# Scans later in their slot, other places for the last weight row and the output chunks, and weight chunks asked for on ScalarE's queue

## The reference, cut to what matters

```python
h = rmsnorm(x, norm_g)
proj = h @ w_in                                  # q, k, v and gate of 3 groups of 8 heads, 8 forget logits
o_sb = stick_breaking_attention(q_sb, k_sb, v_sb)            # group A, strictly causal
o_ch = chunked_attention(rmsnorm(q), rmsnorm(k), v, bias)    # group B, own chunk + 8 before
o_fx = forgetting_attention(rmsnorm(q), rmsnorm(k), v, log_sigmoid(f_logit + b))   # group C, causal
mixed = concat(o_sb * silu(g_sb), o_ch * silu(g_ch), o_fx * silu(g_fx))
out = x + mixed @ w_out
```

## Time and profile before

| | |
|---|---|
| median of 3 runs | 1035.27 us (1034.49 to 1035.57) |
| the profiled execution | 1032.46 us, span 1030.7 us |
| PE busy | 1002.0 us (97%) |
| weight loads of PE | 911.0 us (88%) |
| DVE busy | 702.4 us (68%) |
| ACT busy | 630.4 us (61%) |
| GpSimd busy | 125.9 us (12%) |
| q1, the queue of SP's DMAs | 36.5% of 16 engines' span |

### The profile page before, as it was taken

How to read it: one execution, slowest core, us unless ns; L and a number is a source line. 1 busy time by engine, 2 the same in 40 slices (tenths; PEclk the granted TensorE clock), 3 DMA queues, 4 the chain that set the end, 5 groups by cost and what they waited for, 6 DMA issues and landing times.

```text
span 1030.7 us, 16364 instructions
## 1 busy us (share of the span) xinstructions
PE 1002.0 (97%) x5688; PEld 911.0 (88%) x5688; DVE 702.4 (68%) x1418; ACT 630.4 (61%) x1230; POOL 125.9 (12%) x152
## 2 busy tenths in 40 slices
PE   6999999999999999999999999999999999999998
PEld 6989999899899998898998998998998997787887
DVE  5656685765856867767667757879889888877100
ACT  6676785766766868667767767656566556553000
POOL 1320211101202122112112101002011010000000
PEclk9999999999999999999999999999999999999999
DMA  8244151342431523414315214304304219732920
GB/s 254 84 129 131 29 153 51 82 121 50 121 98 40 152 56 83 123 42 111 96 52 131 74 32 107 78 22 108 77 21 121 73 52 257 202 123 82 346 100 34
DMA packets 118066, 105.51 MB, mean 102 GB/s; under 512 B 10048, under 2 KB 94024, under 8 KB 117984
## 3 DMA queue, kind: packets, MB, share of 16 engines
q1 hardware_dynamic: 115904, 104.43, 36.5%
q10 hardware_dynamic: 2080, 0.04, 0.1%
HBM read 62.44 MB, written 19.98 MB: 80 GB/s over the span
## 4 chain that ended last, share of the span: by engine, by line
PE 75%; DVE 13%; DMA 5%; ACT 3%; issue 2%; SPq 2%; POOL 0%; ACTq 0%; DVEq 0%; POOLq 0%
PE psP L1246 35%; PE psO L1329 7%; PE psP L1250 7%; PE psT L1311 6%; PE psS L1294 4%; PE psS L1295 4%; DVE rb L1150 3%; PE psP L1377 3%; PE psS L1377 3%; PE psP L1347 2%; DMA wraw<-in_w_in_dram 2%; DVE z L1153 2%; PE psO L1377 2%; DVE pt L1161 2%; PE psT L1268 2%
## 5 line engine op out<-in xcount | busy, mean ns | idle before, releaser
L1246 PE MATMUL psP<-big 128*128 128x384 f32 (+1 forms) x2304 | 475.3, 344 | 0.5 <-DVE big L1005 0.5
L1246 PEld LDWEIGHTS psP<-big 128*128 128x128 f32 x2304 | 397.5, 189 | 8.0 <-DVE big L1005 1.0
L1161 DVE TENSOR_TENSOR pt<-psT,pt 128x512 fp32r<-128x512 f32 (+1 forms) x224 | 143.4, 641 | 110.8 <-ACT pt L953 109.6
L953 ACT ACTIVATE pt<-psT 128x512 fp32r<-128x512 f32 (+1 forms) x224 | 124.7, 557 | 103.0 <-PE psT L1311 102.4
L1250 PE MATMUL psP<-big 128*128 128x512 f32 x576 | 156.0, 403 | 0.0
L1329 PE MATMUL psO<-pt,vst 128*128 128x512 f32 (+3 forms) x576 | 138.1, 339 | 12.3 <-DVE pt L1161 11.1
L1311 PE MATMUL psT<-identr,z 128*128 128x128 f32 x816 | 125.6, 273 | 0.0
L1329 PEld LDWEIGHTS psO<-pt,vst 128*128 128x128 f32 x576 | 100.4, 188 | 27.9 <-DVE pt L1161 14.7
L1250 PEld LDWEIGHTS psP<-big 128*128 128x128 f32 x576 | 102.4, 189 | 17.9
L1311 PEld LDWEIGHTS psT<-identr,z 128*128 128x128 f32 x816 | 103.1, 141 | 15.7
L1294 PE MATMUL psS<-stack 128*128 128x256 f32 (+3 forms) x288 | 97.2, 345 | 1.8 <-DVE small L1127 1.8
(11 more groups left out here) (114 smaller groups left out, 1133.4 us busy)
## 6 DMA issues: line engine op xcount, KB each, us to landing
stack<-stack SPq DMA_DIRECT2D x192, 128.0 KB, 2.3
wraw<-in_w_in_dram SPq DMA_DIRECT2D x90, 192.0 KB, 2.7
wraw<-in_w_in_dram SPq DMA_DIRECT2D x24, 256.0 KB, 3.8
mixed_scratch<-mst SPq DMA_DIRECT2D x24, 256.0 KB, 2.7
mixed_scratch<-gate SPq DMA_DIRECT2D x24, 256.0 KB, 3.2
wraw<-in_w_out_dram SPq DMA_DIRECT2D x24, 256.0 KB, 3.2
rb<-decay_scratch SPq DMA_DIRECT2D x8, 512.0 KB, 4.1
big<-mixed_scratch SPq DMA_DIRECT2D x8, 512.0 KB, 5.7
```

Of the source, the lines that this page charges most:

```text
L953: nc.scalar.activation(pt[:, ci % PTR, 0, 0:w], psT[:, m % NT, 0:w], ACT.Copy).then_inc(s_hi, 1)
L1161: nc.vector.tensor_tensor(pt[:, ci % PTR, 1, 0:w], psT[:, m % NT, 0:w], pt[:, ci % PTR, 0, 0:w].bitcast(F32), ALU.subtract).then_inc(s_eva ...
L1246: ins = nc.tensor.matmul(dst[:, 0:TOKW - first], hT[a][:, k, i * P:(i + 1) * P], wpair[b][:, k, first:TOKW], start=(k == 0 and q == 0), st ...
```

## The change

Seven edits, which stand together:

1. ACT issues the DMAs of the chunks from 11 on, in place of SP. At the step of chunk c (c > 8), *ahead of its own copy* of chunk c, it asks for chunk c + 2. The slot's wait stays the same: chunk c + 2 waits for DVE to be done with chunk c - 1. SP keeps the first 11 chunks.
2. The scans of the stick-breaking pairs (`weigh`) stand at 0.92 in place of 0.85.
3. Weights row 7 stands at slot 4.05 in place of 3.6, in pairs 4 to 10.
4. `wout` 6 to 15 start at slot 3.9 in place of 4.2.
5. `forget` 1 stands at slot 6.0 in place of 3.7.
6. `decay` 1 stands at slot 7.0 in place of 4.9.
7. `load_chunk` moves out of SP's program and takes the engine as an argument.

```diff
-AT = {'diag': -0.9, 'tail': 0.3, 'weigh': 0.85, 'recip': 0.9, ...}
+AT = {'diag': -0.9, 'tail': 0.3, 'weigh': 0.85, 'remain': 0.92, 'recip': 0.9, ...}
-BEHIND_TURN = {('weights', 2): 1.5, ('weights', 3): 1.9, ('weights', 4): 2.3}
+BEHIND_TURN = {('weights', 2): 1.5, ('weights', 3): 1.9, ('weights', 4): 2.3, ('weights', 7): 4.05}
-WOUT = [round(0.6 + 0.6 * c, 2) for c in range(SOON)] + [round(4.2 + 0.35 * c, 2) for c in range(EARLY - SOON)]
+WOUT = [round(0.6 + 0.6 * c, 2) for c in range(SOON)] + [round(3.9 + 0.35 * c, 2) for c in range(EARLY - SOON)]
-FORGET = {("forget", 1): 3.7, ("decay", 1): 4.9}
+FORGET = {("forget", 1): 6.0, ("decay", 1): 7.0}
...
-            timed.append((n + AT["weigh"], ("weigh", n)))
+            timed.append((n + AT["weigh" if n < NSOFT else "remain"], ("weigh", n)))
...
+        def load_chunk(c, eng):
...
+            if CPRIOR[c] >= 0:
+                eng.wait_ge(s_wlo, CPRIOR[c] + 1)
+            eng.dma_start(dst, src).then_inc(s_wld[CSLOT[c]], 16)
...
             for step in PLAN:
                 kind = step[0]
-                if kind in ("weights", "gatew", "wout"):
-                    c = CHUNK[step]
-                    if c >= KT:
-                        load_chunk(c + 3)
...
             for step in PLAN:
                 kind = step[0]
+                if kind in ("weights", "gatew", "wout") and CHUNK[step] > KT:
+
+                    load_chunk(CHUNK[step] + 2, act)
```

More of the change, by code:

```diff
@@ L153, in item_cost @@
     return 0
-AT = {'diag': -0.9, 'tail': 0.3, 'weigh': 0.85, 'recip': 0.9, 'rescale': 1.65, 'turn': 1.35, 'turns': 3.05, 'gather': 0.5, 'mix': 2.25}
+AT = {'diag': -0.9, 'tail': 0.3, 'weigh': 0.85, 'remain': 0.92, 'recip': 0.9, 'rescale': 1.65, 'turn': 1.35, 'turns': 3.05, 'gather': 0.5, 'mix': 2.25}
 OWN = {('sq', 1): 0.2, ('norm', 1, 0): 1.0, ('norm', 1, 1): 2.2, ('heads', 0, 1): 1.75, ('keys', 0, 1): 2.4, ('heads', 1, 0): 4.6, ('keys', 1, 0): 5.5, ('keys', 1, 1): 9.5, ('vsplit', 0, 1): 5.6, ('vsplit', 1, 1): 6.6, ('heads', 1, 1): 8.6}
 NEXT = {('weights', 0): 0.2, ('weights', 1): 0.6, ('weights', 2): 1.1, ('weights', 3): 1.6, ('weights', 4): 2.1, ('weights', 5): 2.6, ('weights', 6): 3.1, ('weights', 7): 3.6, ('gatew', 0): 6.3, ('gatew', 1): 7.3, ('sq', 0): 10.3, ('norm', 0, 0): 11.7, ('norm', 0, 1): 12.3, ('heads', 0, 0): 13.4, ('keys', 0, 0): 14.3, ('vsplit', 0, 0): 13.9, ('vsplit', 1, 0): 15.5}
-BEHIND_TURN = {('weights', 2): 1.5, ('weights', 3): 1.9, ('weights', 4): 2.3}
+BEHIND_TURN = {('weights', 2): 1.5, ('weights', 3): 1.9, ('weights', 4): 2.3, ('weights', 7): 4.05}
 KEYS_AT = 0.05
-WOUT = [round(0.6 + 0.6 * c, 2) for c in range(SOON)] + [round(4.2 + 0.35 * c, 2) for c in range(EARLY - SOON)]
+WOUT = [round(0.6 + 0.6 * c, 2) for c in range(SOON)] + [round(3.9 + 0.35 * c, 2) for c in range(EARLY - SOON)]
 FIRST_AT = 3.2
@@ L578, in build @@
         block = ctx.enter_context(nc.Block())
+        def load_chunk(c, eng):
+            if c >= len(CHUNKS):
+                return
+            step = CHUNKS[c]
+            if step[0] == "weights":
+                _, j, k = step
+                g, jj = divmod(ktile(j), PPG)
+                src = w_in[0, k * P:(k + 1) * P, g * 4 * WG:(g + 1) * 4 * WG].rearrange(
+                    "p (f c) -> p f c", f=4)[:, 0:3, jj * P:(jj + 1) * P]
+                dst = wplace[CSLOT[c]][:, 0:QKV].rearrange("p (f c) -> p f c", f=3)
+            elif step[0] == "gatew":
+                _, j, h = step
+                g, jj = divmod(ktile(j), PPG)
+                col = (g * 4 + 3) * WG + jj * P
+                src = w_in[0, h * HALF:(h + 1) * HALF, col:col + P].rearrange("(k p) c -> p k c", p=P)
+                dst = wplace[CSLOT[c]].rearrange("p (k c) -> p k c", k=4)
+            else:
+                pos, half = wout_at(step[1])
+                src = w_out[0, ktile(pos) * P:(ktile(pos) + 1) * P, half * HALF:(half + 1) * HALF]
+                dst = wplace[CSLOT[c]]
+            if CPRIOR[c] >= 0:
+                eng.wait_ge(s_wlo, CPRIOR[c] + 1)
+            eng.dma_start(dst, src).then_inc(s_wld[CSLOT[c]], 16)
@@ L580, in _ @@
         @block.sync
         def _(sp):
[L582 to L604, removed]
@@ L611, in _ @@
             for c in range(KT):
-                load_chunk(c)
+                load_chunk(c, sp)
             for t in range(2, TT):
```

## The result

The changed kernel takes 1045.59 us (median of 4 runs, 1044.83 to 1045.88), the kernel before 1034.88 beside it: ratio 1.0103, 95% interval [1.0089, 1.0116]. It is 10.7 us slower, where the prediction had 2.7. The profiled execution has a span of 1043.6 against 1030.7, so the traces differ by 12.9, of which some 2 us are the low profiled execution of before.

What follows compares the result with a forecast made beforehand. The prediction took the kernel as a PE stream with short stalls, ended by late evacuations. Its terms, +1.6 + 1.9 + 1.2 + 0.3 - 0.6 - 2.1 + 1.2 - 0.8 = +2.7, gave 1035.27 + 2.7 = 1038.0 us; range 1027 to 1041.5.

Steps and rivals of the forecast that it cites:

- The new wait, edit 1: ACT's wait and issue delay its copy and all behind it; SP's heads, keys, mix get earlier, counted as nothing.
- pairs 1 to 3: ACT's chunk copies wait for DVE, mostly in idle time: 0.4 per pair, +1.2 us (0 to 4); pair 4 alike, +0.3.
- Pair 11 (edits 2 and 4): Waits of 1.28 and 1.62 us go; held chunks leave 0.8 of the 2.9; with +2.0 in the tail, net +1.2.
- the cycle: Per chunk where chunks are close: 0.6 (ACT) + 0.65 (DVE) + 0.45 issue + some 0.1 semaphores = 1.8 us.
- Start: Start-up: ACT's copy of the second gate chunk waits for DVE, delaying PE's turn of x block 5: +1.6 us.
- Pair 0: Second copy waits for DVE's first subtraction, moving the first exponential 2.6 us and PE's turn to 64.0: +1.9 us.
- `forget`: `forget` 1 and `decay` 1 moved later: a stall of nearly the same size; gain 0 to 3.4 us, taken as 0.8.
- Forgetting pairs: Pairs 5 to 7: held row 5 copy costs 1.0 each, later row 7 removes PE's last wait; net -0.6 us.
- Pairs 8 to 10: Later scans save 1.5 us a pair, late row 7 hands back 0.5 to 1.0; -2.1 in all (-4.5 to 0).
- Tail: `wout` 16 to 23: each copy waits for DVE, last scan and final unit's turn later: +2.0 us (0 to 3.1).
- 3 (the holds add up): ACT and DVE lock over whole stretches of pair 11 and pairs 1 to 3: +7.4, 1042.7 us; chance 0.15 with another rival.

Runs made afterwards that it cites:

- changed_behind: The changed kernel, with ACT asking for chunk c + 2 behind its own copy of c instead of ahead of it: 1034.7 us, ratio 1.0009 to the kernel before.
- behind_copy: The kernel before with edit 1 alone, but ACT asks for chunk c + 2 behind its own copy of c: 1035.0 us, ratio 1.0008.
- hold_only: The kernel before, loads still on SP; ACT only waits for DVE to finish chunk c - 1 ahead of copying chunk c: 1039.0 us, ratio 1.0046.
- gate_on_sp: The kernel before with edit 1, except that SP still asks for the gate chunks at their old place: 1042.8 us, ratio 1.0081.
- gate_on_act: The kernel before with only the gate chunks asked for by ACT, two ahead; weights rows and `wout` stay on SP: 1045.1 us, ratio 1.0109.
- queue_only: Also called the queue alone: the kernel before with edit 1 and none of the new places: 1048.3 us, ratio 1.0134.
- times_only: The changed kernel with its chunk loads given back to SP, three ahead, all new places kept: 1029.0 us, ratio 0.9950 to the kernel before.
- wout_on_sp: The kernel before with edit 1, except that the `wout` chunks stay with SP: 1044.8 us, ratio 1.0103.
- wait_ahead_issue_behind: The kernel before with edit 1, the wait for DVE ahead of ACT's copy and only the DMA put behind it: 1038.4 us, ratio 1.0047.
- row7_scans_split: The kernel before, loads on SP; row 7 at 4.05 in forgetting pairs, 3.88 in pairs 8 to 10, scans at 0.92 there: 1023.2 us, ratio 0.9900.

## Why the prediction was wrong

The sign was right and the size was not. changed_behind parts the run into what the request's place ahead of the copy costs (the change less changed_behind) and all the rest (changed_behind less before). The prediction's terms part the same way: 12.1 for waits and issue ahead (in pair 11 the 2.0 of the tail and the 2.1 of gain that it let the loop take), and -9.4 for the new places.

| | start | 0 | 1 to 3 | 4 | 5 to 7 | 8 to 10 | 11, tail | sum |
|---|---|---|---|---|---|---|---|---|
| place ahead, predicted | +1.6 | +1.9 | +1.2 | +0.3 | +3.0 | 0 | +4.1 | +12.1 |
| measured | -0.2 | +2.1 | +1.2 | +0.7 | +3.1 | +0.4 | +4.5 | +11.8 |
| the rest, predicted | 0 | -0.8 | 0 | 0 | -3.6 | -2.1 | -2.9 | -9.4 |
| measured | +1.1 | +0.1 | +3.7 | +0.8 | -2.3 | -3.9 | +1.7 | +1.2 |

The sum for the place ahead came out (12.1 and 11.8), in part by luck: the 4.5 of pair 11 has 1.7 us of low clock in it that no term had, and at the start the wait is there in both kernels. Of the rest, the near fit in pairs 5 to 10 is not the prediction's mechanism: behind_copy has -2.2 and -3.6 there with none of the new places. And the rest of pair 0 is flattered by the low clock of before, 1.7 us. The loss that the prediction lacked came in two steps.

- *"What is behind SP's queue (heads, keys, mix) gets earlier, which no wait of PE asks for: I give it nothing."* This step of "The new wait, edit 1" failed. The queue was also an order: a chunk asked for behind the key copies in the same queue did not make them late. From a second queue it does, and the copies, with 1.06 us of slack, take 1.8 longer. That is the 3.7 of pairs 1 to 3: behind_copy has 3.3 with no wait ahead of the copy, hold_only has 0.1, gate_on_sp takes 1.0 a pair away in pairs 2 and 3, and gate_on_act brings it back alone. The 0.8 of pair 4 is not of this kind: in changed_behind the key copy is in time there, and hold_only has the same 0.8 without any load moved. In pair 11 the step shows as the wait for `mixF`, 2.70 us, of which 1.81 is still there in changed_behind. That one takes both edits: it is 0.75 with the queue alone, and 0 in times_only and in behind_copy.
- *Pair 11 (edits 2 and 4)*. I took 2.9 us of waits as removed by the new places. Those two waits do go in the changed kernel, but others come in their place, whoever loads: with SP's loads (times_only) 0.74 and 0.33 are left of them, and there are new ones of 1.75 us before `scores` 183, for a sigmoid of ACT's, and of 1.83 for a later evacuation, so that pair 11 is 2.2 longer than before and not 2.9 shorter. `wout` from 3.9 alone puts 3.37 us before the bank of the earlier trace rows that had 1.62. With the queue alone, the move of `wout` is most of the loss there (5.0, and 1.1 in wout_on_sp).

In the same paragraph of the prediction one attribution was wrong too. I took the in-order wait as the cost and the issue as a small part of the cycle. By wait_ahead_issue_behind, measured with the old places, it is the other way: 9.0 us for the issue ahead of the copy, 4.0 for the wait.

The rest, by the prediction's terms:

- *Start* (+1.6): right by the wait; the stage itself is not resolved. PE's turn of block 5 waited 1.43 us, 1.00 in hold_only. In changed_behind 0.92 of it stays, since there the wait holds what stands behind the copy.
- *Pair 0* (+1.9): the chain was right, PE's turn at 64.87 with a wait of 1.66, and 64.0 was forecast. The hold is its cause: hold_only has that wait too (1.19). Its stage ends level only because its clock stayed up where before's fell; without those 1.7 us it is 1.6 longer.
- *`forget`* (-0.8): a stall nearly as large came, 0.98 and 0.39 us before two later steps where 1.81 was, and the clock stayed up.
- *Forgetting pairs* (-0.6): +0.8. The cost of 1.0 each was right; the gain was 2.3 instead of 3.6, though times_only has the whole of it (-4.1). Against queue_only the new places gain 1.8 in these pairs and 2.6 in pairs 8 to 10.
- *Pairs 8 to 10* (-2.1): -3.5, inside its bounds. The wait for row 7 was 0.32 us in pairs 8 and 10 and under 0.1 in pair 9, where 0.5 to 1.0 was handed back. The stretch that answers to the earlier trace rows, 219.80 us in place of 223.50:

```profile
630.60:850.40 219.80, 218.16 (x1273) 200.35 (x1272) 186.97 (x248) 141.67 (x261) 17.29 (x18) 1.00 0.29 73
```

- *Tail* (+2.0): right in place, somewhat low; waits of 1.28 and 1.70 stand before two `end` steps, where before had one of 0.2.

Of the rivals, 3 (the holds add up) had the right sign by the wrong cause. By the Trainium skill (Perfetto Trace Analysis, section on the HWDGE DMA instruction) a DMA's semaphore wait is done by the sequencer. The trace agrees: in pair 6 DVE ends at 496.44, the DMA goes out at 496.48, and ACT, idle for 1.44 us until then, starts the copy behind it at 496.96. By the Trainium skill (DMA: Bandwidth & Descriptors, Issuing engines are not separate DMA queues) DMAs of all issuing engines run on the same 16 DMA engines and interleave, and another issuer saves only the sequencer's time. The trace agrees with both halves: over 200 to 211 us before and 206 to 216 us after the DMAs moved 192 and 196 GB/s, and the 128 KB copy shared them with the other queue's load. The prediction took from this rule that there is no bandwidth to gain, and passed over the interleaving: what changed was who lands first.

Open: the 0.8 of pair 4, which the wait alone makes, and how pair 11 divides. Of its +6.2, 1.7 is the clock; the waits behind it shift from run to run.

## What to carry to other kernels

A queue that an engine issues on is an order: before moving transfers off it, list what stood ahead of them there, with the slack of each, and keep large loads behind the small copies that PE waits for. If an in-order engine must issue a load, put the request behind its own work, where the issue runs beside it; one place ahead made 10 us of 1035. When two places are moved towards each other, look at the step between them: row 7 and the scans gain separately, and together only when row 7 stays ahead of the scan.

## What the runs showed of the hardware

- A DMA issued on ACT's sequencer takes 0.37 us (374/374/463 ns over 109), as on SP, and is hidden beside a running copy of 0.62, but not ahead of it.
- A DMA can be held up by one of another queue that was issued after it: a 128 KB copy issued 0.10 us before a 256 KB load of the other queue landed after 4.1 us. With a 192 KB load 0.65 us behind it in its own queue it took 2.4.
- Not every gap of PE is followed by a low clock. The same 1.81 us gap in pair 0 was followed by a granted clock of 0.60 in the trace of before, and by 1.00 in that of row7_scans_split (columns as in the earlier trace rows). Where it falls, it costs about 1.7 us here, as much as the gap itself:

```profile
79.00:83.00 4.00, 4.00 (x29) 3.92 (x28) 3.93 (x9) 2.95 (x7) 0.00 (x0) 1.00 0.49 135
```
